# A two-layer diffusion backbone on one core: the modulation stage is split over the first norm, the MLA preparation and the output stage

## The reference

```python
for l in range(DEPTH):                       # DEPTH = 2
    mod_x = (silu(c) @ w_ada[l] + b_ada[l])[:, None, :]      # w_ada: (2, 1024, 6144)
    mod_c = silu(c_ctx) @ w_ada[l] + b_ada[l]
    sh1, sc1, ga1, sh2, sc2, ga2 = split(mod_x, 6)
    csh1, csc1, cga1, csh2, csc2, cga2 = split(mod_c, 6)
    z_x = (rms_norm(x, g_norm1[l]) * (1 + sc1) + sh1) @ w_in[l]      # z_c the same with csc1, csh1
    ...                                      # four head groups on z: conv, MLA, RWKV-7, retention
    x = x + ga1 * (concat(y) @ w_out[l])
    h = rms_norm(x, g_norm2[l]) * (1 + sc2) + sh2
    x = x + ga2 * expert_choice_moe(h)       # 16 experts; context tokens the same with the c* rows
```

## Time and profile before

| | us |
|---|---|
| median of three runs | 5423.49 |
| the profiled execution | 5427.15 |
| its span | 5425.1 |
| TensorE busy | 4421.1 (81%) |
| VectorE busy | 1522.5 (28%) |
| ScalarE busy | 822.2 (15%) |
| matmuls of the modulation (L212) busy | 166.3 |

### The profile page before, as it was taken

How to read it: one execution, slowest core, us unless ns; L and a number is a source line. 1 busy time by engine, 2 the same in 40 slices (tenths; PEclk the granted TensorE clock), 3 DMA queues, 4 the chain that set the end, 5 groups by cost and what they waited for, 6 DMA issues and landing times. The chain is left out here.

```text
span 5425.1 us, 61712 instructions
## 1 busy us (share of the span) xinstructions
PE 4421.1 (81%) x26628; PEld 2332.7 (43%) x26628; DVE 1522.5 (28%) x3047; ACT 822.2 (15%) x1754; POOL 446.5 (8%) x662
## 2 busy tenths in 40 slices
PE   8799958846687659999999699958748678399998
PEld 1364523335473324444444364523337454244444
DVE  0210252266653340000000210262176642500000
ACT  0100022213331100000100200022222321000000
POOL 0000010002120000000000000010012110000000
PEclk9899959968798879999999799969869789699999
DMA  8411000010003245555554221000010021588885
GB/s 310 135 57 67 6 25 0 0 53 18 15 3 114 107 154 221 223 214 206 205 205 171 76 71 58 1 25 0 30 39 3 14 80 66 207 304 305 309 308 189
DMA packets 215533, 623.71 MB, mean 115 GB/s; under 512 B 37848, under 2 KB 48216, under 8 KB 214744
## 3 DMA queue, kind: packets, MB, share of 16 engines
q1 hardware_dynamic: 194200, 546.99, 27.2%
q0 software_dynamic: 21056, 72.69, 4.6%
q10 hardware_dynamic: 8, 0.10, 0.0%
HBM read 565.83 MB, written 53.90 MB: 114 GB/s over the span
## 5 line engine op out<-in xcount | busy, mean ns | idle before, releaser
L1935 PE MATMUL ps<-moe_w,e_xT 128*128 128x512 f32 x2048 | 890.4, 595 | 2.2 <-ACT e_xT L1995 2.2
L1935 PEld LDWEIGHTS ps<-moe_w,e_xT 128*128 128x128 f32 x2048 | 389.4, 191 | 500.0 <-issue 497.0
L418 PE MATMUL ps<-hT,p_w 128*128 128x512 f32 (+1 forms) x1344 | 486.0, 525 | 19.7 <-DMA p_w<-in_w_in_dram 19.7
L1935 PE MATMUL ps<-moe_w,e_hT 128*128 128x512 f32 x1024 | 448.0, 595 | 35.9 <-ACT e_hT L2012 35.9
L421 PE MATMUL ps<-p_w,hT 128*128 128x272 f32 (+1 forms) x1280 | 422.3, 492 | 0.0
L418 PEld LDWEIGHTS ps<-hT,p_w 128*128 128x128 f32 x1344 | 258.0, 192 | 246.5 <-issue 213.3
L421 PEld LDWEIGHTS ps<-p_w,hT 128*128 128x128 f32 x1280 | 243.2, 190 | 178.9 <-issue 154.0
L1742 PE MATMUL ps<-o_w,yT 128*128 128x512 f32 x576 | 286.1, 660 | 30.4 <-DMA o_w<-in_w_out_dram 24.4
L1935 PEld LDWEIGHTS ps<-moe_w,e_hT 128*128 128x128 f32 x1024 | 191.9, 190 | 273.1 <-issue 229.6
L2029 DVE TENSOR_TENSOR e_hid<-e_hid,ps 128x512 f32<-128x512 f32 x64 | 44.0, 687 | 847.2 <-PE ps L1935 847.2
L2039 DVE SCALAR_TENSOR_TENSOR e_ye<-ps,all_gate,e_rows 128x1024 f32<-128x1024 f32 (+1 forms) x48 | 61.4, 1280 | 651.3 <-PE ps L1935 515.7
(11 more groups left out here) (309 smaller groups left out, 5497.0 us busy)
## 6 DMA issues: line engine op xcount, KB each, us to landing
moe_w<-in_w_gate_dram SPq DMA_DIRECT2D x64, 2048.0 KB, 16.9
moe_w<-in_w_up_dram SPq DMA_DIRECT2D x64, 2048.0 KB, 12.3
moe_w<-in_w_down_dram SPq DMA_DIRECT2D x64, 2048.0 KB, 17.9
mod_wa<-in_w_ada_dram SPq DMA_DIRECT2D x24, 2048.0 KB, 8.0
p_w<-in_w_in_dram SPq DMA_DIRECT2D x10, 2048.0 KB, 8.2
z_rows<-p_zo POOLq DMA_DIRECT2D x40, 256.0 KB, 2.3
r_z<-z_rows SPq DMA_DIRECT2D x20, 512.0 KB, 3.3
h_rows<-o_h POOLq DMA_DIRECT2D x18, 512.0 KB, 3.0
```

The source lines that it names most:

```text
L418: ins = nc.tensor.matmul(ps[:, j % NB, 0:tw], w[:, n % RW, k, m * P:(m + 1) * P], hT[:, k, t0:t0 + tw], start=(k == 0), stop=(k == KT - 1))
L1935: return nc.tensor.matmul(ps[0:cap, b, :], xs[:, kk, 0:cap], rhs, start=(kk == 0), stop=(kk == KT - 1))
```

## The change

There is no modulation stage any more. What it computed is made in three places, all in layer 0:

- `stage_norm1` of layer 0 computes shift and scale directly as columns: four loads of 2 MB of `w_ada` (columns 0 to 2047), and for each of 16 column blocks of 128 eight matmuls with the weights as the stationary operand (128x128) and the condition as the moving one (2 columns), 128 matmuls in all, before the first transposes. VectorE adds the bias in one instruction and makes G, between tile 0 and tile 1. The condition and the bias are loaded as columns. The evacuations wait for G, and ScalarE's squares no longer do.
- `stage_mla_prep` of layer 0 makes rows 2 to 5 of layer 0 through `ModRows`: 8 loads of 2 MB (two k-tiles x 2048 columns each, rows of 8 KB) in two slots, and after `heads(t-1)` of iteration t the matmuls of load t-2, eight of them, with the condition padded to 32 columns as the stationary operand, to the four partition quarters of one PSUM bank. Two bias additions, eight small stores.
- `stage_out` of layer 0 makes all six rows of layer 1 in the same way: 12 loads, one product of eight matmuls after the transposes of each tile, the last three after those of the last tile; three bias additions and twelve small stores. Its router product and its small transpose move together into PSUM bank 7.

```diff
-        stage_modulation(nc, g, I)
+MOD_PREP = [(0, 2 * D), (0, 4 * D)]
+MOD_OUT = [(1, 0), (1, 2 * D), (1, 4 * D)]
+MOD_LOADS = 4
...
+    def load(self, sp, j):
+        l, c0 = self.blocks[j // MOD_LOADS]
+        k0 = 2 * (j % MOD_LOADS)
+        if j >= 2:
+            sp.wait_ge(*self.summed.at(j - 1))
+        sp.dma_start(self.w[:, j % 2].rearrange("p k q n -> p k (q n)"),
+                     self.I["w_ada"][l].rearrange("(k p) f -> p k f", p=P)[:, k0:k0 + 2, c0:c0 + 2 * D]).then_inc(*self.w_in[j % 2].up(16))
+
+    def product(self, pe, j):
+        b, part = divmod(j, MOD_LOADS)
+        pe.wait_ge(*self.w_in[j % 2].at(16 * (j // 2 + 1)))
+        if part == 0 and b:
+            pe.wait_ge(*self.used.at(b))
+        for k in range(2):
+            kk = 2 * part + k
+            for q in range(4):
+                ins = self.nc.tensor.matmul(self.g.ps[32 * q:32 * q + 32, self.bank, :], self.g.cond[:, kk], self.w[:, j % 2, k, q],
+                                            start=(kk == 0), stop=(kk == KT - 1))
+        ins.then_inc(*self.summed.up())
...
+    def store(self, sp, b):
+        l, c0 = self.blocks[b]
+        sp.wait_ge(*self.used.at(b + 1))
+        for q in range(4):
+            sp.dma_start(self.g.mod[l, :, c0 + 512 * q:c0 + 512 * q + 512], self.rows[32 * q:32 * q + 2, b]).then_inc(*self.stored.up(16))
...
 def stage_norm1(nc, g, I, l):
+                for j in range(NW if first else 0):
+                    if j >= RW:
+                        sp.wait_ge(*mm.at(j - RW + 1))
+                    sp.dma_start(wa[:, j % RW], I["w_ada"][l].rearrange("(k p) f -> p k f", p=P)[:, :, j * 512:(j + 1) * 512]) \
+                        .then_inc(*wa_in[j % RW].up(16))
...
+                if first:
+                    pe.wait_ge(*silu_done.at(1))
+                    for j in range(NW):
+                        pe.wait_ge(*wa_in[j % RW].at(16 * (j // RW + 1)))
+                        for i in range(4):
+                            n = 2 * (4 * j + i)
+                            for k in range(KT):
+                                ins = nc.tensor.matmul(ps[:, 4, n:n + 2], wa[:, j % RW, k, i * P:(i + 1) * P], g.cond[:, k, 0:2],
+                                                       start=(k == 0), stop=(k == KT - 1))
+                        ins.then_inc(*mm.up())
                 for t in range(NT):
                     pe.wait_ge(*normed.at(t + 1))
...
 def stage_mla_prep(nc, g, I, l, S):
                     sp.dma_start(z[:, t % 3], g.zt[t * P:(t + 1) * P, 0:W_MLA]).then_inc(*z_in[t % 3].up(16))
+                    if mod and t == 2:
+                        mod.load_bias(sp)
+                        mod.load(sp, 0)
+                    if mod and 2 <= t < mod.n + 1:
+                        mod.load(sp, t - 1)
+                if mod:
+                    for b in range(len(MOD_PREP)):
+                        mod.store(sp, b)
+                    sp.wait_ge(*mod.stored.at(64 * len(MOD_PREP)))
...
                     if t >= 1:
                         heads(t - 1)
+                    if mod and t >= 2:
+                        mod.product(pe, t - 2)
                 heads(NT - 1)
...
 def stage_out(nc, g, I, l, need_ctx):
+                    if mod:
+                        for j in range(n, n + 1) if n < len(tiles) - 1 else range(n, mod.n):
+                            mod.product(pe, j)
                     pe.wait_ge(*te.at(n + 1))
```

More of the change, by code:

```diff
@@ L163, in row @@
     return v.partition_broadcast(P)
[L166 to L222, removed]
-                    s = slice(n * 512, (n + 1) * 512)
-                    nc.vector.tensor_tensor(mo[:, s], ps[0:2, j % 4, :], ba[:, l, s], ALU.add).then_inc(*used.up())
-        sg.settle()
@@ L241, in stage_norm1 @@
         G = sb("G", [P, 2, KT])
+        first, NW, RW = l == 0, 4, 3
+        if first:
+            wa = sb("wa", [P, RW, KT, 512])
+            cc = sb("cc", [P, KT, 2])
+            ba = sb("ba", [P, 2, KT])
+        wa_in, silu_done, mm = [sg(f"mod_in{i}") for i in range(RW)], sg("silu_done"), sg("mod_mm")
         x_in, small, sq, normed = [sg(f"w_slot{i}") for i in range(3)], sg("small_in"), sg("sq_done"), sg("normed")
@@ L255, in _ @@
                     sp.dma_start(xb[:, t % 3], g.x_rows(I, l, t)).then_inc(*x_in[t % 3].up(16))
+            n_coef = 3 if first else 2
             def evac_act(act, t):
                 act.wait_ge(*tr.at(2 * t + 1))
+                if t == 0:
+                    act.wait_ge(*coef.at(n_coef))
                 s = 1 if t < NCT else 0
@@ L266, in _ @@
             def _(act):
-                act.wait_ge(*coef.at(2))
+                if first:
+                    act.wait_ge(*small.at(80))
+                    act.wait_ge(*coef.at(1))
+                    nc.scalar.activation(g.cond[:, :, 0:2], cc[:], ACT.Silu).then_inc(*silu_done.up())
                 for t in range(NT):
@@ L675, in _ @@
                     norm_rotate(t)
+                    if mod and t in (5, 9):
+                        mod.add_bias(dve, t // 4 - 1)
             @block.gpsimd
@@ L1716, in _ @@
                     sp.dma_start(xi_[:, n % 2], g.x_rows(I, l, t)).then_inc(*x_in[n % 2].up(16))
+                    if mod and n == 1:
+                        mod.load_bias(sp)
+                        mod.load(sp, 0)
+                    if mod and n >= 1:
+                        mod.load(sp, n)
+                if mod:
+                    for j in range(len(tiles), mod.n):
+                        mod.load(sp, j)
+                    for b in range(len(MOD_OUT)):
+                        mod.store(sp, b)
+                    sp.wait_ge(*mod.stored.at(64 * len(MOD_OUT)))
             @block.gpsimd
```

69 lines of the change are left out of this document (56 added, 13 removed).

## The result

| | before | after |
|---|---|---|
| median of the runs | 5425.43 us (4 runs, 5422.89 to 5428.14) | 5366.22 us (4 runs, 5365.38 to 5378.84) |
| span of the profiled execution | 5425.1 | 5363.4 |
| its mean granted TensorE clock | 0.889 | 0.890 |

What follows compares the result with a forecast made beforehand. The modulation stage, bound by both TensorE and DMA, holds up everything behind it. Start -148, MLA preparation +68, output stage +26 make -54: 5427.15 becomes 5373, median about 5370; own range 5355 to 5385, wider range 5325 to 5405.

Steps and rivals of the forecast that it cites:

- the mechanism: First norm: weight loads, not the 2 columns, set the products' pace, transfers hide; 226.9 us becomes about 79, gain 148.
- rival A: First norm: column products stay at half clock, 57.6 us instead of 30.4, +27, total 5397; chance 0.15.
- 256 x 0.113 = 28.9 us: First norm: 256 records of the column products at 0.113 us each, the pace of a product with 32 columns.
- the ring: MLA preparation: product, z behind weights, squares, cT, key/value product, heads, product; 18.1 us a turn, six turns add 63.
- the ends: MLA preparation: last product, partly hidden, and closing bias addition and four stores outside the turns; 5 us for both.
- Rival B: MLA preparation: bursts 7.5 us long raise the clock, a turn is 14.4 us; -25, total 5345; chance 0.18.
- Rival C: MLA preparation: z is not held up by the whole load, lands after 2.7 us; -38, total 5332; chance 0.13.
- Served in turn: MLA preparation: z waits for the whole 2 MB load ahead of it, landing 9.1 us after the weights' issue.
- The tail's +14.5: Output stage, last tile: products 9 to 11 and the wait for load 11 delay the router product by 14.5 us.
- The end, 6: Output stage, behind the softmax: bias addition, four stores and their landing, 0.7 + 2.5 + 2.7 = 6 us.
- 0.7 x 9 = 6: Output stage, tiles 0 to 8: a 1.8 us product replaces a 1.10 us TensorE wait, 0.7 more each.
- Rivals D and E: D: start's column records don't overlap, 0.48 us each, +93, 5463; chance 0.05. E: turns and tail eat all 148; 0.03.

Runs made afterwards that it cites:

- Experiment 5: Changed kernel with 18 matmuls of 384 columns ahead of the first norm's column products, while the first weights load; 5362.32 us, one run.
- experiment 4: Changed kernel with the first norm's column products moving 32 columns of the padded condition instead of 2; 5377.8 us, one run.
- experiment 2: Changed kernel with z of tiles 4 to 9 in the MLA preparation issued by ScalarE on its own queue; 5345.16 us, one run.

## Why the prediction came out as it did

**The total was right because two errors of opposite sign met.** The first stage gained 20.6 less than forecast; the other two cost 18.1 and 11.8 less. That is 9.3 in favour, less 1.5 in stages that nobody touched: 54 + 9.3 - 1.5 = 61.8, where the spans differ by 61.7. Between the medians it is 59, since the profiled execution of before lay 1.7 above its median of four runs and that of the changed kernel 0.8 below. That the sum came within 4 us of the forecast is luck, then: the parts miss by 12 to 21 each.

**The start: the mechanism held, the size was that of rival A.** "256 x 0.113 = 28.9 us" is the failed step. The pace of a record was taken from a product at full clock. Measured were 0.214, close to the 0.225 of the half-clock row that was named as the other bound. The term came to 54.74 instead of 30.4, +24.3; the weights landed 2.3 earlier than forecast and the rest was 1.1 shorter. Experiment 5 shows that this is the clock, and experiment 4 that the columns have no part in it. The argument against rival A was that RWKV's small matmuls ran at 0.96. It failed because it compared busy shares: experiment 5 has TensorE busy without a gap and the clock down. Rival A's price, +27, was nearly right (+24.3); its total, 5397, was not, because the other two terms were too dear. What the transfers needed was hidden, as forecast.

The Trainium skill, "TensorEngine Tiling (Array Packing)", Instruction Overhead, makes a matmul with one column cost what one with sixty costs. The trace agrees for 2 against 32 columns (54.74 and 54.79 us).

**The MLA preparation: the ring held, with two terms too large.** The turn was forecast as 9.2 + 1.4 + 2.1 + 1.9 + 3.5 = 18.1 and came as 8.2 + 1.4 + 1.9 + 1.5 + 2.7 in the one shown, 15.6 on average. (The 9.2 is 9.1 in the prediction's own working; the 0.1 plays no part.) 1.0 of the difference is z's landing, 0.6 key/value product and heads, and 0.8 the product (1.2 by the six turns' average of 2.3), since the clock rises in the burst. Six turns 2.5 shorter are 15 us; the other 3 are the ends, 2.0 for 5. Rival B had foreseen this rise and put it over the whole turn, 14.4; it came only in the second half of each burst. So the truth lay between forecast and B. Rival C fell: z was held up. But the reason given for it was only partly right. "Served in turn" was read from two loads of one queue; experiment 2 shows that a third of the delay is the queue's order, and that two thirds stay when z has a queue of its own and runs beside the load.

The Trainium skill, "DMA: Bandwidth & Descriptors", Queues, rings and completion order, says that queues take turns on an engine packet by packet. I had made 3 to 4 us of it for z on a queue of its own, and a turn of 12 to 13. The run has 6.0 and 13.6: the direction is right, and the gain from a second queue is less than that estimate.

**The output stage: right in the tail, too dear in the tiles.** The tail's +14.5 came as +13.0. Two terms were too large, and a third difference is no term at all. The end, 6, took 2.85: the bias addition came behind the softmax as forecast (0.67), but the four stores were issued in 1.12 us where 2.5 had been read from four loads of single elements, and the next block began 1.4 after the last issue, not 2.7. And "0.7 x 9 = 6" came as 1.4 in sum, and as -0.3 to +2.6 over the seven traces with this output stage: the product (1.92) took the place of a wait of 1.10, but the fastest tile is 20.2 now and 20.8 before. The third is the head, 3.0 shorter, of which 2.7 are its two projections (15.78 and 14.00 us at a higher granted clock, 16.81 and 15.70 before). That is no merit of the change: without it the stage would have cost 17. Whether the filled gap itself keeps the clock up in the next projection is suggested by that and not shown. The change of tiling mode on both sides cost nothing that the rows show (1632.71 + 1.04 against 1633.67, and 1633.67 + 1.92 against 1635.53).

**Rivals D and E** had no part: the records overlapped, and of the 127.4 gained at the start 61.7, about half, were left. E's price was also mis-added: to eat the remaining 54 us, six turns and the tail would have needed some 8 more each, not 12.

## What to carry to other kernels

Count weight loads before columns: a small product over a large matrix costs the number of 128x128 tiles that the matrix makes as the stationary side, and a quarter of that when it is the moving side, even with the transposes that follow (256 records against 64 for the same 8 MB here). When work is put into the gaps of another stage, draw the ring that its transfers close: a load whose issue waits for a product holds up everything small that is asked for after it, and asking for the small transfer one turn earlier gave back 45 of 50 us where another queue gave 12. And leave a tail no loads: the three products and one load behind the last transposes cost 15.8 us, and the same products cost 4 to 9 in earlier tiles.

## What the runs showed of the hardware

- TensorE fell from 2.4 to 1.2 GHz while it was busy without a gap with fp32 weight loads of 128x128 and 2 moving columns (0.50 with 20.00 of 20.00 us busy, experiment 5), and didn't rise in the 46 us that were left of the stream. With 32 columns the stream took the same time. A busy TensorE is thus no sign of a full clock.
- In the changed kernel's trace the granted clock reads 1.00 over records that come at 0.214 us, the pace that reads 0.50 in experiment 5, where changes of the clock are recorded ahead of it; in the kernel before it reads 1.00 over 3 us at half pace. At the start of a kernel the pace of the records is the better clock.
- A transfer of 272 KB beside one of 2 MB took 6.0 us on its own queue, 7.7 behind it in the same queue, and 2.7 alone.
- The same 32 matmuls took 13.90 to 16.67 us within one stage, with the clock as the only difference seen. Untouched stages move with it from one execution to the next: layer 0's attention took 296.6 us at a mean granted clock of 0.92 and 305.4 at 0.88.
